# A fused transformer block on one core: the in-projection summed in six K parts of 1, 1, 1, 2, 1, 2 pairs of tiles in place of five of 1, 1, 2, 2, 2

## What is computed

```python
# S = 256 tokens, D = 2048, FF = 8192, fp32
mod = silu(c) @ w_ada + b_ada              # six vectors of D: shift, scale, gate for mixer and MLP
h = rms_norm(x, norm_mix) * (1 + sc_a) + sh_a
p = h @ w_in                               # the in-projection, 2048 x about 4096
...                                        # latent, stick-breaking and forgetting attention, 8 heads each
x = x + g_a * (o @ w_out)
h = rms_norm(x, norm_ffn) * (1 + sc_m) + sh_m
x = x + g_m * (square(relu(h @ w_ff1)) @ w_ff2)
return rms_norm(x, final_norm)
```

## Time and profile before

| | us |
|---|---|
| three runs | 1168.31, 1135.22, 1165.99 (median 1165.99) |
| profiled execution | 1139.96 |
| its span | 1138.2 |
| PE, PEld busy in it | 1100.8, 1067.6 |
| DVE, ACT, POOL busy | 720.1, 532.7, 315.3 |
| DMA | 296.88 MB, mean 261 GB/s |

### The profile page before, as it was taken

One profiled execution on the slowest core, in us unless ns is written; L12 is line 12 of the kernel. 1 busy time (PEld: TensorE's weight loads), 2 busy tenths in 40 slices (PEclk: granted clock), 3 DMA queues, 4 the chain that ended last, 5 costly groups with the idle time before them and its releaser, 6 DMA issues.

```text
span 1138.2 us, 21704 instructions
## 1 busy us (share of the span) xinstructions
PE 1100.8 (97%) x9084; PEld 1067.6 (94%) x9084; DVE 720.1 (63%) x924; ACT 532.7 (47%) x674; POOL 315.3 (28%) x157
## 2 busy tenths in 40 slices
PE   7889999999998999999999999999999999999996
PEld 6779999997798989999999999999999999999995
DVE  4588868788865569877776444545555555445453
ACT  4644454676563344544544434343544444344441
POOL 3997997866048960000000000000000000000001
PEclk9999999999999999999999999999999999999998
DMA  9999999998659977888786665666666666656651
GB/s 362 408 390 398 395 375 368 366 361 298 232 187 383 342 285 278 301 305 288 273 280 200 190 199 189 197 193 199 188 195 195 196 189 195 199 190 193 195 184 74
DMA packets 81888, 296.88 MB, mean 261 GB/s; under 512 B 9088, under 2 KB 9216, under 8 KB 81792
## 3 DMA queue, kind: packets, MB, share of 16 engines
q1 hardware_dynamic: 81792, 295.50, 73.6%
HBM read 293.37 MB, written 2.10 MB: 260 GB/s over the span
## 4 chain that ended last, share of the span: by engine, by line
PE 81%; DMA 6%; DVE 3%; POOL 3%; ACT 3%; issue 3%; SPq 0%; DVEq 0%; ACTq 0%
PE ps L1402 48%; PE ps L1408 24%; DMA ada<-in_ada 4%; PE ps L1420 3%; POOL w_lo L840 2%; PE ps L1589 2%; DMA raw<-in_weights 1%; PE ps L1425 1%; DVE ada L965 1%; ACT w_hi L486 1%; PE ps L1599 0%; POOL ssq L834 0%; ACT o_tok L747 0%; PE ps L1555 0%; PE ps L1554 0%
## 5 line engine op out<-in xcount | busy, mean ns | idle before, releaser
L486 ACT ACTIVATE w_hi<-raw 128x1024 fp32r<-128x1024 f32 x346 | 363.4, 1060 | 440.2 <-PE ps L1408 357.8
L946 DVE TENSOR_TENSOR w_lo<-raw,w_hi 128x1024 fp32r<-128x1024 f32 x254 | 308.8, 1224 | 267.1 <-ACT w_hi L486 266.7
L1402 PE MATMUL ps<-hT,w_hi 128*128 128x256 f32 x3072 | 381.7, 277 | 9.4 <-ACT w_hi L486 3.2
L1402 PEld LDWEIGHTS ps<-hT,w_hi 128*128 128x128 f32 x3072 | 364.3, 188 | 12.7 <-issue 6.4
L1402 PE MATMUL ps<-act,w_hi 128*128 128x256 f32 x2048 | 252.9, 276 | 0.0
L1402 PEld LDWEIGHTS ps<-act,w_hi 128*128 128x128 f32 x2048 | 241.6, 188 | 0.0
L840 POOL TENSOR_TENSOR w_lo<-raw,w_hi 128x1024 fp32r<-128x1024 f32 x92 | 219.7, 2408 | 55.0 <-ACT w_hi L486 54.7
L1408 PE MATMUL ps<-hT,w_lo 128*128 128x256 f32 x1536 | 206.6, 277 | 0.9 <-DVE w_lo L946 0.6
L834 POOL TENSOR_TENSOR ssq<-ssq,sq 128x1024 f32<-128x1024 f32 x6 | 14.4, 2401 | 657.3 <-ACT sq L493 657.3
L1408 PEld LDWEIGHTS ps<-hT,w_lo 128*128 128x128 f32 x1536 | 189.4, 188 | 1.3 <-DVE w_lo L946 0.8
L1408 PE MATMUL ps<-act,w_lo 128*128 128x256 f32 x1024 | 136.9, 276 | 0.0
(11 more groups left out here) (228 smaller groups left out, 821.2 us busy)
## 6 DMA issues: line engine op xcount, KB each, us to landing
raw<-in_weights SPq DMA_DIRECT2D x346, 512.0 KB, 4.3
ada<-in_ada SPq DMA_DIRECT2D x180, 512.0 KB, 6.2
more<-in_weights SPq DMA_DIRECT2D x16, 512.0 KB, 8.6
more<-in_ada SPq DMA_DIRECT2D x12, 512.0 KB, 8.5
xT<-in_xt SPq DMA_DIRECT2D x4, 512.0 KB, 7.0
y<-tmp SPq DMA_DIRECT2D x4, 256.0 KB, 2.5
consts<-in_consts SPq DMA_DIRECT2D x1, 580.0 KB, 12.7
y<-sq SPq DMA_DIRECT2D x2, 256.0 KB, 3.0
```

What stands on the lines that cost most here:

```text
L486: sc.activation(w_hi[:, slot, :, :], raw_room(u0 + j), ACT.Copy).then_inc(hi_done, 1)
L946: ve.tensor_tensor(w_lo[:, slot, :, :], raw_room(u), w_hi[:, slot, :, :].bitcast(F32), ALU.subtract).then_inc(lo_vec, 1)
L1402: pe.matmul(acc[:, n, :], w, rhs[:, kt0 + k, half, :], start=first and k == 0 and n % 2 == 0 and half == 0, stop=False, skip_group_check=True)
```

## The change

PARTS goes from five parts to six. Parts 0 and 1 stay units 0 to 7 and 8 to 15; part 2 is now units 16 to 23 (pair 2), part 3 units 24 to 39 (pairs 3 and 4), part 4 units 40 to 47 (pair 5), part 5 units 48 to 63 (pairs 6 and 7). ADA_STOPS gets a row for each of the six parts: part 1 now works off tiles 19 to 28, part 2 tiles 29 to 39, part 3 tiles 40 to 53, part 4 tiles 54 to 63; part 5 has the tiles of the old part 4. Gains and operands of a coming single pair are made in blocks 5 and 6, those of a coming two in blocks 3 and 4, and 6 and 7. POOL makes the low half of pair 2 before unit 18 and that of pair 3 before unit 24. The c_rep copies move to part 3. The numbers of the PSUM uses that follow grow by 8. The weight units are laid out in memory in the order in which they are used.

```diff
--- before.py
+++ after.py
@@ -54,8 +54,8 @@
 SH_A, SC_A, G_A, SH_M, SC_M, G_M = range(6)
 
 
-PARTS = (1, 1, 2, 2, 2)
-PART_AT = (0, 1, 2, 4, 6, 8)
+PARTS = (1, 1, 1, 2, 1, 2)
+PART_AT = (0, 1, 2, 3, 5, 6, 8)
 BLOCKS = 8
 V_BLOCKS = (4, 7)
 A_GA, A_SHM, A_SCM, A_GM, A_END = 64, 96, 128, 160, 192
@@ -70,7 +70,7 @@
 WIDE, RAWS = 5, 6
 A_WIDE = A_GA - A_GA % WIDE
 U_WIDE = 48
-MIX_POOL = {10: 1, 16: 2, 19: 3}
+MIX_POOL = {10: 1, 18: 2, 24: 3}
 
 
 def ada_of(a):
@@ -122,17 +122,17 @@
     return u // RAWS + 1 if u < U_WIDE else U_WIDE // RAWS + (u - U_WIDE) // RING + 1
 
 
-ADA_STOPS = ((8, 9, 10, 12, 14, 16, 17, 18, 19), (19, 21, 23, 25, 27, 30, 32, 32, 32),
-             (32, 35, 38, 41, 44, 46, 48, 48, 48), (48, 51, 54, 57, 60, 62, 64, 64, 64),
-             (64, 67, 70, 73, 75, 78, 80, 83, 86))
+ADA_STOPS = ((8, 9, 10, 12, 14, 16, 17, 18, 19), (19, 20, 21, 22, 23, 24, 26, 27, 29),
+             (29, 30, 31, 32, 35, 38, 40, 40, 40), (40, 41, 43, 45, 47, 48, 50, 52, 54),
+             (54, 55, 56, 56, 59, 62, 64, 64, 64), (64, 67, 70, 73, 75, 78, 80, 83, 86))
 
 
 USE_XS = 0
 USE_IN = 1
-USE_LST = 37
-USE_OUT = 42
-USE_FFN = 46
-USE_FF1A, USE_FF2A, USE_FF1B, USE_FF2B, USE_END = 47, 55, 59, 67, 71
+USE_LST = 45
+USE_OUT = 50
+USE_FFN = 54
+USE_FF1A, USE_FF2A, USE_FF1B, USE_FF2B, USE_END = 55, 63, 67, 75, 79
 
 READY_XS, READY_ROT, READY_FFN, READY_END = 1, 2, 3, 4
 
@@ -580,7 +580,7 @@
             for p, n in enumerate(PARTS):
                 for b in range(BLOCKS):
                     if p + 1 < len(PARTS):
-                        if b == (7 if p else 6):
+                        if b == (6 if PARTS[p + 1] == 1 else 7):
                             mix_operand(PART_AT[p + 2] - 1)
                         if b == 4 and PARTS[p + 1] == 2:
                             mix_operand(PART_AT[p + 1])
@@ -1111,15 +1111,15 @@
                 for b in range(BLOCKS):
                     todo = list(ada_in_part(p, b))
                     if not last:
-                        if p == 0 and b == 5:
-                            mix_gain(1)
-                        if p and b == 3:
+                        if PARTS[p + 1] == 1 and b == 5:
                             mix_gain(PART_AT[p + 1])
-                        if p and b == 6:
+                        if PARTS[p + 1] == 2 and b == 3:
+                            mix_gain(PART_AT[p + 1])
+                        if PARTS[p + 1] == 2 and b == 6:
                             mix_gain(PART_AT[p + 2] - 1)
                     for a in todo[:1]:
                         ada_tile(a)
-                    if p == 2 and b >= 6:
+                    if p == 3 and b >= 6:
                         h = b - 6
                         ve.tensor_copy(c_rep[:, h * D // 2:(h + 1) * D // 2], crep_ps[h]).then_inc(c_kept, 1)
                     if last and b == 4:
@@ -1129,7 +1129,7 @@
                     if not last:
                         if b == 4 and PARTS[p + 1] == 2 and PART_AT[p + 1] not in MIX_POOL.values():
                             mix_lo(PART_AT[p + 1])
-                        if b == (7 if p else 6) and PART_AT[p + 2] - 1 not in MIX_POOL.values():
+                        if b == (6 if PARTS[p + 1] == 1 else 7) and PART_AT[p + 2] - 1 not in MIX_POOL.values():
                             mix_lo(PART_AT[p + 2] - 1)
                     if last and b == 2:
                         ve.tensor_scalar(fx, pT[0:H, T_F, :], cols[0:H, C_BF:C_BF + 1], None,
```

## The result

The changed kernel takes 1149.65 us (median of 11 runs, 1146.16 to 1176.69); the kernel before, run beside it on the same chip, 1140.49 (median of 11, 1135.22 to 1168.31). The runs of this program fall on two levels, some 27 us apart, and the ratio of the two kernels, 1.0094 with a 95% interval of 1.0077 to 1.0110, is taken from the runs of the lower level alone: a real loss of 0.9%. The profiled execution took 1150.96 us (span 1149.1) against 1139.96 (span 1138.2): +11.0.

What follows compares the result with a forecast made beforehand. TensorE's stream was taken to bound the kernel; -4.4 (part 1), +6.0 (part 2), +7.5 (part 4) and +0.5 (clock) gave +9.6 us, added to the median 1165.99 for 1175.6 us (ratio 1.008), range 1140 to 1182.

Steps and rivals of the forecast that it cites:

- What bounds it: Whole kernel: the last chain is 81% TensorE, so a microsecond off TensorE's stream counts unless a transfer takes it back.
- Part 1: Units 8 to 15: waits for VectorE go, GpSimd's low half of pair 2 holds unit 16 until 77.9; 4.4 us won.
- Part 2: Units 16 to 23: VectorE's gains, tiles and adds make TensorE wait 2.35, 2.35 and 1.15; +6.0 us in the sum.
- Part 3: Units 24 to 39: VectorE's work hidden, but pair 5's low half at 2.1 us makes unit 41 wait 0.6.
- Part 4: Units 40 to 47: waits of 1.35, 4.4 and 1.2 behind tiles and pair 6's low half; +7.5 with part 3's 0.6.
- 0.5 for the clock: Behind the 4.4 us wait in part 4: one slow unit, 1.7 us less 1.2 of waiting it replaces.
- The sum: Whole kernel: -4.4 + 6.0 + 7.5 + 0.5 = +9.6 us, ratio 1.008; 1149.6 by the profile, 1175.6 by the median.
- the first rival: Parts 1 and 4: low halves take 0.69, pair 2's is early; part 4 loses 4.5, part 1 wins 5.7; chance 0.15.
- Hidden bursts: VectorE's low halves or tiles hardly delay adds: +4, or the whole gain stands, 1136 or 1162 us; chance 0.15.
- the transfer that takes up the delay: Ada transfer at 240.36 us and its like land when they do now, so all 9.6 vanish: 1140 or 1166; chance 0.12.
- late tiles: Blocks 4 of parts 2 and 4: tiles may come 2 us after VectorE wants them, +4, 1154 or 1180; chance 0.13.
- repeatedly: Parts 1, 2 and 4: single-pair waits keep dropping TensorE's clock, units take 4.41 not 2.73, 1180 or 1206; chance 0.05.

Runs made afterwards that it cites:

- the first experiment: The changed kernel with four ada tiles moved from part 4 to part 3, at most one per block left in part 4; ratio 1.0034 to the kernel before.
- the best order: The changed kernel with tiles of parts 1 to 4 spread and pair 2's low half before unit 17; ratio 1.0009 to the kernel before.
- the 23 equal pauses of the MLP: The kernel before, with TensorE waiting for its own last matmul ahead of each later MLP product; 1157.68 to 1162.21 us, one run 1173.70.

## Why the prediction was right in the change and wrong in the time

**What bounds it**: right. All that was lost or won came through TensorE's stream, and nothing after unit 48 gave it back.

**Part 1** (-4.4): -4.7. Unit 16 was given as 77.9 and came at 77.40, for the reason named, the low half behind GpSimd's unbroken row. Not foreseen was that TensorE would be early enough (units 8 to 13 at 2.72 to 2.80 each) for an idle stretch of 2.58, behind which the clock fell: unit 16 took 4.44. In the profile of the first experiment, with the same code up to there, it was unit 8 that was slow (4.43), and unit 16 came at 77.40 all the same.

**Part 2** (+6.0): +6.8. Waits of 2.35, 2.35 and 1.15 were forecast; start to start the units 20 to 22 exceed their 2.75, 2.72 and 2.72 by 1.35, 2.36 and 1.16. The first is 1.0 short because unit 16, slow by 1.7 us, had already cost that time; the size of the sum is right here partly by luck. Unit 24: 105.7 forecast, 105.93 measured.

**Part 3** (0, with 0.6 pushed into part 4): +1.3, and a step that was missing. There was no wait; TensorE worked at its slow pace, 2.83 a unit. The low half took 1.89, within the bounds given. VectorE ended part 3 at 153.02, 2.1 us into unit 40 and not 3.2: the copies of c_rep took 1.14 from start to start, not 1.48, and the slow pace gave it room. The run with the low half before unit 17 had part 3 at the fast pace and no wait at unit 41 either.

**Part 4** (+7.5, and 0.5 for the clock): +7.0. Start to start, units 44 and 45 are 1.25 and 3.6 us over, and unit 46 took 4.40. The low half took 1.43, at the lower row and not at the mean of 2.1; the trace of the kernel before has one more such row, 1.13 us at 109.73, which the mean left out. One slow unit behind the long wait, in the place of block 7's: as forecast. The three errors, low half, pace and the 0.6 that didn't come, cancel, and that is luck.

**The sum**: +9.6 forecast, +10.15 at unit 48, +11.0 in the profiled execution, 9.2 between the medians, 1.0094 as a ratio where 1.008 was forecast. The medians mix the levels (4 of 11 runs and 1 of 11 on the upper); 1.0094 of the lower level is 10.7 us. Two slips in the working changed nothing: the 178.8 given for unit 48 leaves out the 0.5 for the clock, and in the first rival part 4 would by its own terms lose about 5.6 and not 4.5.

**The level**: wrong, and the one step that failed. "Two of three being on the upper, I add the sum to the median." Three runs can't tell how often a level comes, and the profile, the only execution that showed its inside, was on the lower one. The runs showed that the levels are 27 us apart because TensorE holds one pace or the other through 256 units of the MLP, and that the share of the upper one changes with no change of the kernel: 4 of 11 runs of the kernel before beside the result, and 5 of 23, 11 of 18 and 6 of 17 in three sessions on chips 9, 13 and 4. Which pace a run enters the MLP with was not found, so no forecast of the level could have been more than a draw; on the second of those chips the upper one would have been the better guess. The rows of before held a hint: units 9 and 10 take 5.68 us together, 2.84 each, where the units from 16 on take 2.73. The difference times 256 is 28 us, about the distance of the levels. The forecast should have been 1149.6 with the upper level as a rival at 1175.6.

**Rivals.** Hidden bursts, the transfer that takes up the delay, and late tiles didn't happen: every wait of parts 2 and 4 ended at L1033, and +11.0 was still there at 1134 us. The clock fell at two places, one unit each (0.81 granted from 75 to 80 us, 0.67 from 172 to 177), and not repeatedly, and no other profile has more than two slow units between 8 and 48. What the Trainium skill says of short idles between groups (TensorE: Matmul & The Clock Gate, section "A second HAM failure mode: psum-queue depth-cycling"), weighed there, came true only in so far as a wait of 2.58 and one of 3.42 brought the clock down for a unit.

## What to carry to other kernels

A finer split along K to start earlier pays with one drain (the add that empties PSUM) per block, and in a block that is as short as its drain plus one other job, everything that the draining engine has queued ahead of the drain is paid at full price: count its work block by block, not per stage, and spread it before judging the split. Fill the slack of long blocks with work that must be done before the short ones. Even then the split won nothing here: the best order came out at 1.0009 (0.9993 to 1.0026). Before a forecast is made in absolute time, find out which execution the profile is, and what the runs' levels are made of.

## What was not expected of the hardware

**Two paces of TensorE at one clock.** 24 matmuls of 256 columns with their weight loads take 2.72 or 2.83 us while the granted clock reads 1.00. In these profiles the pace changes only where TensorE resumes behind a wait (also a very short one) or at a unit with other shapes, and then holds: in the kernel before through the three double parts at 2.72, after the change through part 3 at 2.83. At the 23 equal pauses of the MLP it changed every time, from one pace to the other. What sets it was not found.

**The clock behind a wait.** Waits of 2.05 to 2.07 us were followed by a slow unit in some runs (pair 6's low half on GpSimd: 0.66 granted, 4.46 us) and by none in others (unit 22 after the change, 2.07). The 2.58 before unit 16 was followed by 4.44 us, 2.62 at the same place in the run with pair 6's low half on GpSimd by none. One of 3.38 us, in the run with the low half before unit 17, was followed by none, one of 3.42 by 4.40 us. A wait's length alone did not decide it.
